# Four of the sixteen chunks of the first two modulation strips multiplied on TensorE with a column of silu(c)

## The reference

```python
c_act = jax.nn.silu(c)                              # (1, 1024)
for l in range(DEPTH):
    mod = c_act @ mod_w[l] + mod_b[l]               # (1, 6 * 1024)
    sh1, sc1, g1, sh2, sc2, g2 = jnp.split(mod, 6, axis=-1)
    h = modulate(x, norm_g[l, 0], sh1, sc1)         # rmsnorm(x) * g * (1 + sc1) + sh1
    y = gla_mixer(h, ...) if l < n_a else swa_sink_attention(h, ...)
    ...
```

## Time and profile before

| | us |
|---|---|
| runs of before (three) | 2585.71, 2585.95, 2589.53 |
| their median | 2585.95 |
| the profiled execution, span from first to last instruction | 2591.7 |
| difference of that span to the median | 5.75 |
| TensorE busy in that span | 2514.7 (97%) |
| VectorE busy | 2119.7 (82%) |
| ACT busy | 1220.0 (47%) |
| mean granted TensorE clock | 0.990 of full |

### The profile page before, as it was taken

One profiled execution on the slowest core, in us unless ns is written; L12 is line 12 of the kernel. 1 busy time (PEld: TensorE's weight loads), 2 busy tenths in 40 slices (PEclk: granted clock), 3 DMA queues, 4 the chain that ended last, 5 costly groups with the idle time before them and its releaser, 6 DMA issues.

```text
span 2591.7 us, 48983 instructions
## 1 busy us (share of the span) xinstructions
PE 2514.7 (97%) x17184; PEld 2192.0 (85%) x17184; DVE 2119.7 (82%) x3783; ACT 1220.0 (47%) x1769; POOL 468.9 (18%) x385
## 2 busy tenths in 40 slices
PE   5999999999999999999999999999999999999998
PEld 4789999888888877899998888887878789777987
DVE  7889997888888778869978888887777788777754
ACT  4544444545444545444444554444545554334543
POOL 2115992000000001018980000000101000110000
PEclk8999999999999999999999999999999999999999
DMA  9775555555456887365555445546887567964554
GB/s 345 259 263 168 179 178 172 166 166 185 169 167 211 284 271 272 130 220 171 183 179 166 162 166 185 170 168 231 282 286 256 189 222 262 318 242 163 171 183 149
DMA packets 147831, 538.38 MB, mean 208 GB/s; under 512 B 16609, under 2 KB 16865, under 8 KB 147442
## 3 DMA queue, kind: packets, MB, share of 16 engines
q1 hardware_dynamic: 114226, 414.78, 46.9%
q0 software_dynamic: 32752, 119.24, 13.2%
q10 hardware_dynamic: 720, 2.62, 0.3%
HBM read 533.42 MB, written 3.15 MB: 207 GB/s over the span
## 4 chain that ended last, share of the span: by engine, by line
PE 83%; DVE 7%; POOL 3%; issue 3%; DMA 2%; ACT 2%; SPq 0%; DVEq 0%; POOLq 0%; ACTq 0%
PE ps L2003 26%; PE ps L1529 9%; PE ps L2748 7%; PE ps L748 6%; PE ps L1505 6%; PE ps L1457 5%; PE ps L1533 5%; PE ps L2730 5%; PE ps L1948 3%; PE ps L1509 3%; POOL split_lo L1575 3%; PE ps L2734 2%; DVE gate L928 1%; DMA gate<-in_mod 1%; PE ps L2142 1%
## 5 line engine op out<-in xcount | busy, mean ns | idle before, releaser
L1562 ACT ACTIVATE split_hi<-ring 128x1024 fp32r<-128x1024 f32 x760 | 801.0, 1056 | 757.8 <-PE ps L1509 199.8
L1587 DVE TENSOR_TENSOR split_lo<-ring,split_hi 128x1024 fp32r<-128x1024 f32 x572 | 698.5, 1222 | 177.0 <-ACT split_hi L1562 172.2
L1575 POOL TENSOR_TENSOR split_lo<-ring,split_hi 128x1024 fp32r<-128x1024 f32 x128 | 339.9, 2672 | 91.2 <-ACT split_hi L1562 90.9
L1559 ACT ACTIVATE gate_hi<-gate 128x256 fp32r (+1 forms) x252 | 105.4, 418 | 405.4 <-PE ps L2003 398.9
L2003 PE MATMUL ps<-split_hi,gate_hi 128*128 128x512 f32 x1024 | 285.1, 398 | 1.5 <-DVE gate_lo L1585 1.5
L2003 PE MATMUL ps<-split_hi,gate_lo 128*128 128x512 f32 x1024 | 278.2, 392 | 5.1 <-DVE gate_lo L1585 5.0
L2003 PE MATMUL ps<-split_lo,gate_hi 128*128 128x512 f32 x1024 | 278.0, 391 | 0.0
L1505 PE MATMUL ps<-h_parts,split_hi 128*128 128x256 f32 x2048 | 266.9, 283 | 0.0
L1529 PE MATMUL ps<-h_parts,split_hi 128*128 128x512 f32 x1024 | 261.6, 397 | 0.0
L1505 PEld LDWEIGHTS ps<-h_parts,split_hi 128*128 128x128 f32 x2048 | 254.9, 192 | 0.0
L2003 PEld LDWEIGHTS ps<-split_hi,gate_lo 128*128 128x128 f32 x1024 | 192.6, 189 | 48.4 <-DVE gate_lo L1585 7.5
(11 more groups left out here) (405 smaller groups left out, 3951.0 us busy)
## 6 DMA issues: line engine op xcount, KB each, us to landing
ring<-in_stream SPq DMA_DIRECT2D x776, 512.0 KB, 4.3
small<-in_mod POOLq DMA_DIRECT2D x104, 512.0 KB, 5.6
mod_w<-in_mod POOLq DMA_DIRECT2D x64, 512.0 KB, 5.2
gate<-in_mod POOLq DMA_DIRECT2D x44, 512.0 KB, 6.9
gate<-in_mod SPq DMA_DIRECT2D x8, 512.0 KB, 16.2
gate<-in_mod ACTq DMA_DIRECT2D x4, 512.0 KB, 8.3
x_kept<-x POOLq DMA_DIRECT2D x8, 256.0 KB, 3.9
gate<-x_kept POOLq DMA_DIRECT2D x4, 512.0 KB, 8.5
```

The source lines that it names most:

```text
L1562: nc.scalar.activation(split_hi[:, e, :], ring[:, slot, e * D:(e + 1) * D], ACT.Copy).then_inc(hi_made, 1)
L1575: nc.gpsimd.tensor_tensor(split_lo[:, e, :], ring[:, slot, e * D:(e + 1) * D], split_hi[:, e, :].bitcast(F32), ALU.subtract).then_inc(lo_m ...
L1587: nc.vector.tensor_tensor(split_lo[:, e, :], ring[:, (START[name] + j) % RING, e * D:(e + 1) * D], split_hi[:, e, :].bitcast(F32), ALU.sub ...
```

## The change

Shift chunks 4 to 7 of the first layer are no longer multiplied by VectorE. The host lays them out transposed, in eight blocks of 128 inputs by 128 outputs. ACT makes a second silu(c), as a column per block (`c_col`, [128, 8]), from eight more columns of the `cols` input; it waits for `cols` between L553 and L554 to do so. TensorE multiplies each block, as stationary weights, with one column of `c_col`, eight products added up in one column of PSUM per chunk. VectorE adds the bias to that column (`shift_bias_vector`) and counts up `first_mod_used`, at the place where the chunk's product stood. On TensorE, chunk 4 stands ahead of the gl products, chunk 5 ahead of gl product 0, chunk 6 ahead of gl product 2, chunk 7 ahead of gl product 4. Chunk 7 shares PSUM bank 7 with chunk 4 and waits until ten chunks are done.

```diff
+SHIFT_ON_VECTOR = 4
...
+        c_col = sb("c_col", [P, 8])
...
+        SHIFT_BANK = {4: 7, 5: 5, 6: 6, 7: 7}
+
+        def shift_chunk_tensor(t, c):
+
+            t.eng.wait_ge(shift_landed[c], 16)
+            t.wait_ge(*when("c_col"))
+            if c == 7:
+                t.eng.wait_ge(first_mod_used, 10)
+            w = shift_mod[:, c, :].rearrange("p (k n) -> p k n", k=DC)
+            for k in range(DC):
+                ins = nc.tensor.matmul(ps[:, SHIFT_BANK[c], c:c + 1], w[:, k, :], c_col[:, k:k + 1],
+                                       start=(k == 0), stop=(k == DC - 1))
+            ins.then_inc(tensor_steps, t.step(f"shift.full{c}"))
+
+        def shift_bias_vector(v, c):
+            v.wait_ge(*when(f"shift.full{c}"))
+            s = PLACE[MOD1[0] + SH1]
+            nc.vector.tensor_tensor(modc[:, s, c:c + 1], ps[:, SHIFT_BANK[c], c:c + 1], mod_b(s, c), ALU.add) \
+                .then_inc(first_mod_used, 1)
...
             nc.scalar.activation(c_row, c_row, ACT.Silu).then_inc(scalar_steps, a.step("c_act"))
+            a.eng.wait_ge(cols_landed, 16)
+            nc.scalar.activation(c_col[:, :], col("cond"), ACT.Silu).then_inc(scalar_steps, a.step("c_col"))
             nc.scalar.activation(c2_row, c2_row, ACT.Silu).then_inc(scalar_steps, a.step("c2_act"))
...
             for c in range(DC):
                 if c >= 4:
                     scale_chunk_vector(v, c)
-                shift_chunk_vector(v, c)
+                if c < SHIFT_ON_VECTOR:
+                    shift_chunk_vector(v, c)
+                else:
+                    shift_bias_vector(v, c)
...
+            shift_chunk_tensor(t, 4)
             for c in range(DC):
+                if c % 2 == 0 and 5 + c // 2 < DC:
+                    shift_chunk_tensor(t, 5 + c // 2)
                 t.wait_ge(*when(f"n1.T{c}"))
                 ins = nc.tensor.matmul(ps[0:16, 4, 0:SEQ], gla_wgl[:, c, :], hT[:, c, :], start=(c == 0), stop=(c == DC - 1))
...
+    for n in range(PLACE[MOD1[0] + SH1] * DC + SHIFT_ON_VECTOR, PLACE[MOD1[0] + SH1] * DC + DC):
+        mod[n] = mod[n].T.reshape(DC, P, P).transpose(1, 0, 2).reshape(P, D)
```

More of the change, by code:

```diff
@@ L109 @@
 for _name, _n in [("mod_b", STRIPS * 8), ("norm1", 32), ("kvn1", 8), ("fin", 8),
-                  ("norm2", 64), ("kvn2", 8), ("b_g2", 4), ("qn", 3), ("kvl", 2), ("pos", 4)]:
+                  ("norm2", 64), ("kvn2", 8), ("b_g2", 4), ("qn", 3), ("kvl", 2), ("cond", 8), ("pos", 4)]:
     COLS[_name] = N_COLS
@@ L3284, in pack @@
         vec(g["norm_g_2"], 8), vec(g["kv_norm_2"], 8), vec(g["gla_b_g2"], 4), vec(g["b_q_norm_2"], 3),
-        vec(g["kv_lora_norm_2"], 2)], axis=1)
+        vec(g["kv_lora_norm_2"], 2), vec(g["c"], 8)], axis=1)
     inv1 = f(500000.0) ** (-np.arange(0, 2 * ROT1, 2, dtype=f) / f(2 * ROT1))
```

## The result

The changed kernel takes 2602.15 us (median of 9; 2595.44 to 2608.56) beside 2586.96 (9; 2584.67 to 2599.78): 1.0045 times the kernel before, interval 1.003 to 1.0061, so 7.8 to 15.8 us. The sign and the mechanism are as forecast; the measured median lies 3.65 us above the range. Measured again beside other kernels it was 2597.96 (12; 2592.89 to 2604.52): 1.004 (1.003 to 1.0051), 7.8 to 13.2 us.

A forecast was written before the change was run, and what follows sets the result against it. Two strands bounded the start: VectorE, ACT, TensorE to 34.96 us, and POOL's inputs to 35.77. TensorE's queue moves the glT copy +8.1 us, less 0.6 for the clock: net +7.5, 2593.5 us, range 2586.5 to 2598.5.

The forecast's parts named there:

- The sign and the mechanism: Whole kernel slower, net +7.5 us, because chunk products on TensorE delay the glT copy from 35.80 to 43.95 us.
- The path: First 45 us: TensorE's queue ends last and releases the glT copy at 43.95 us, no longer the inputs.
- Their price: Chunk products on TensorE: 16 records a chunk, 1.8 us at full clock (0.114 each), 3.4 at half (0.21 each).
- the nearest row: L2472, 128x128 f32 blocks with 8 columns, 0.114 us a record at full clock, taken as the one-column products' price.
- the bounds 1.2 and 5.3: Half-clock chunk price: at least 1.2 us from bf16 records, at most 5.3 us with weights loads that nothing hides.
- chunk 4: 23.98 + 1.8 = 25.8, about all of it at full clock: First step of TensorE's queue: chunk 4 starts at 23.98 us, takes 1.8 us, before the clock falls at about 25.6.
- 4.6 to 4.8 us: Delay from the last close or wide matmuls to the clock's fall, put after transposes ending at 20.93: about 25.6 us.
- Granted is the full 2.4 GHz until about 28.7 us: Clock reading of the kernel before: full until about 28.7 us, then half, 1.2 GHz, until about 45.8.
- the credit of 0.6 us: In `gla_qk`: half clock lasts 4.6 us in place of 5.8, saving 0.6 us.
- rival 2: First 45 us: clock stays full; copy +0.65, z -1.9, `gla_qk` -2.9, together -4.1 us, 2581.8 us; chance 0.12.
- Rivals 1, 3 and 4: Clock falls only at 28.7, +5.7 us (0.10); chunk at bf16 price, +0.9 (0.10); weights load not hidden, +13.2 (0.06).
- the anchor: Median time of the kernel before, 2585.95 us, to which the forecast difference of +7.5 us was added.

The follow-up runs named there:

- e2: Changed kernel with gl products 0 to 3 put ahead of chunks 4 and 5 on TensorE, the rest interleaved; 1.0025 times the kernel before.
- e1: Changed kernel without the TensorE products of shift chunks 4 to 7, which are the bias alone; 1.0001 (0.999 to 1.0012) times the kernel before.
- e11: Changed kernel with each chunk's eight products done twice, 64 in place of 32; 1.0094 (1.008 to 1.0107) times the kernel before.
- e6: Kernel before with unread identity products on TensorE ahead of gl products 4 to 7 and of z; 1.0004 (0.9991 to 1.0017) times the kernel before.
- e5: Changed kernel with unread identity products on TensorE ahead of chunk 4 and between the one-column products; 1.0024 times the kernel before.
- e7: Changed kernel with weights and column of chunks 4 to 7 read as bf16 upper halves; 0.9996 (0.9984 to 1.0008) times the kernel before.
- e9: Changed kernel with only chunks 4 and 5 on TensorE, behind gl product 3, and inputs issued early; 1.0007 (0.9994 to 1.0019) times the kernel before.
- e8: Kernel before with POOL issuing its five small inputs at the eighth product, not the twelfth; 0.9998 (0.9988 to 1.0007) times the kernel before.

## Why the prediction was right, and where it failed

**Right.** The path: the copy released by TensorE, 16 records a chunk. Their price: 3.50 us at half clock against 3.4, 1.95 against 1.8 at full (e2); the nearest row was the right one, the bounds 1.2 and 5.3 were not needed. Gl products 1.81 a pair of c against 1.8. VectorE's idle 13.4 us, over 10. ACT's second silu (0.21 us at 8.84) ends in the shadow of x, awaited to 12.60, and e1 shows that this, the longer `cols` and the new layout together cost nothing that its interval (0.999 to 1.0012) can tell. That a delay before the glT copy reaches the end: e11.

**The step that failed: "chunk 4: 23.98 + 1.8 = 25.8, about all of it at full clock".** The clock did not fall at about 25.6. The stretches of the changed kernel around the start of chunk 4 (24.28), columns as before:

```profile
23.00:24.00 1.00, 0.00 (x0) 0.00 (x0) 0.84 (x2) 0.87 (x2) 0.00 (x0) 0.95 1.02 414
24.00:25.00 1.00, 0.72 (x4) 0.75 (x4) 0.00 (x0) 0.00 (x0) 0.00 (x0) 0.50 1.04 426
...
54.00:55.00 1.00, 1.00 (x8) 1.00 (x7) 0.94 (x3) 0.34 (x2) 0.00 (x0) 0.69 0.92 311
```

A clock of 0.95 over 23 to 24 us and 0.50 behind it is a fall at 23.9, before the first product; in the second profiled execution the same stretch shows

```profile
23.00:24.00 1.00, 0.00 (x0) 0.00 (x0) 0.60 (x2) 0.63 (x2) 0.00 (x0) 0.72 0.98 401
```

so still sooner, about 23.4. Both chunks then ran at half clock, 6.96 us, to 31.2 in place of 29.8. I had carried 4.6 to 4.8 us over from two places where TensorE went on with a few narrow products; here the transposes ended at 20.8 and it did nothing at all until the load landed, 3.48 us by the timeline's bracket. When other products stood in that gap, chunk 4 was at full clock (e2: 1.95 us). That the idle wait is the cause is not shown, though: e11, whose TensorE does the same up to chunk 4, had its fall only at 24.9, inside the chunk,

```profile
24.00:25.00 1.00, 0.68 (x6) 0.71 (x7) 0.00 (x0) 0.00 (x0) 0.00 (x0) 0.96 1.05 430
```

and e0, the kernel before once more, had it 3.7 us after the eight gl records (23.93 to 27.67) where the sum carried over 4.8. With the same work ahead of it the moment moves by more than a microsecond, so it could not be taken from one execution. Behind this lies a reading that failed, "Granted is the full 2.4 GHz until about 28.7 us". The column reads 1.00 from the start on, but the durations do not: the 16 transposes took 3.76 us in before and 3.49 in the second execution of the changed kernel, where the last two records start 0.11 us apart and those ahead of them 0.19 to 0.31. So the clock was at half through most of the transposes and rose only about when they ended, or later; why it fell again so soon stays open.

Of the 1.5 us by which the copy is late (45.49 against 43.95; 45.29 in the second execution) 1.4 stem from here, and chunks 6 and 7 add 0.1 each.

**Twice too large: the credit of 0.6 us** for the clock's return inside `gla_qk`. The half-clock stretch there went from 49.69 to about 54.6 (0.69 over 54 to 55 in the stretches above), 4.9 us in place of 4.6, which by the same working gives 0.4; the chain gives `gla_qk` 24.46 us in place of 24.76, 0.3 less. e6 shows that little more is to be had: with the clock full it waits for gla_lo and for ACT's splits. For the same reason rival 2's -2.9 for `gla_qk` was no gain that e5 or e6 found. Its -1.9 for z came, and most of it was still there at the first `gla_v` product (63.85 us in e6, 65.42 in before, with the copy 0.3 sooner); it went between 113 and 137 us (see Open), and e6's time is 1.0004. The side that rival 2 stood on did not come with a full clock. The Trainium skill, "TensorE: Matmul & The Clock Gate", section "Why this matters for your kernels", advises to leave no idle gaps between bursts of matmuls; e6 filled most of them and had the full clock, without a gain: right behind z TensorE was not what ended last.

**Rivals 1, 3 and 4** fall by the rows: the clock fell sooner, not later; 0.22 us a record is neither the bf16 row's nor that of a weights load that nothing hides. A cheap record came only with bf16 data (e7).

**The range.** With the copy and the credit as measured the working gives 8.1 + 1.5 - 0.3 = 9.3 us (the traces show 9.1 and 9.3 at the PEER query), so 2595.3 on the median given, inside the range. So of the 8.65 us between forecast and measured median, 1.8 are the clock and the credit. The other 6.85, which put it outside the range, lie within the spread of single executions and of the anchor (1.0 of them is the anchor: 2586.96 for nine runs against 2585.95 for three). The second comparison's median, 2597.96, is inside. Medians of the kernel before are 2585.95, 2586.96, 2587.38, 2589.47, 2590.92 and 2591.42, and single executions of it go from 2581 to 2600. Three runs had put the anchor at the low end, and the range had no term for it. What makes single executions differ is settled in part only. The mean granted clock goes with it: in the three groups of 35, 35 and 29 executions of before, the median of those with 0.991 or more lies 4.9 to 6.3 us below that of those with 0.989 or less; in e0's twelve it is 2.3 us. Two profiled spans of the same kernel, 2591.7 and 2585.1, are only 0.5 us apart at the PEER query, so most of it arises later: some 6 us of it between 1780 and 1800 us, where the first of them has TensorE busy for 4.01 of 6 us and then a clock of 0.57 over 8 us, and the second is busy throughout at 1.00.

**Open.** Why the clock fell at 23.4 to 24.9 us, as said. Why e2, e5 and e6 lose some 1.6 us between 113 and 137 us. In e6 the clock falls for a short time there,

```profile
116.00:120.00 4.00, 4.00 (x15) 2.97 (x13) 3.50 (x8) 0.46 (x2) 0.00 (x0) 0.71 0.00 0
```

where the kernel before has 1.00. In e2 and e5 it falls there too (0.65 and 0.61 over 122 to 124 us), and none of the other eleven profiled executions has either the fall or the loss; that the one causes the other was not tried. An exact version that beats the kernel before was not found.

## What to carry to other kernels

Work moved to an engine that looks free in a stretch is priced in that engine's queue: here 32 one-column products stood in front of the products that the path needs, and an f32 product with weights of its own costs about the same for 1 column (0.122 us a record) as for 64 (0.115). Before crediting the relief of the other engine, ask what ends beside it: VectorE's 4.5 us were worth 0.5 at the copy until the inputs moved too. And take neither the clock of a new stretch nor an anchor from few executions: with the same work ahead of it the clock fell at 23.4, 23.9 and 24.9 us, three runs put the median 1.0 to 5.5 us below those of larger groups, and durations are to be read beside the clock column.

## What the runs showed of the hardware that was not expected

- In e2 the clock fell at 27.0 us while TensorE was nearly always busy with one-column f32 products (a single gap of 0.16 us since 24.34). In e5, with pairs of 128-column products between them, it stayed full from 24 to 43 us.
- The granted clock reads 1.00 ahead of its first recorded change whatever the pace. In e9:

```profile
21.50:25.25 3.75, 3.63 (x9) 1.13 (x9) 2.06 (x5) 1.29 (x3) 2.71 (x5) 1.00 1.03 419
```

The eight gl records in it took 3.59 us, 0.45 each, the pace of half clock; the same eight took 1.92 in e2, where everything ahead of them on TensorE is the same, and 3.59 again in e8, also at 1.00. In e7 the column reads 1.00 up to 35 us, over gl products at 1.89 us for four. The Trainium skill, on the page named above, section "What's actually happening", says that the number of slow products at a kernel's start varies from run to run of one kernel; these runs agree with that, and durations tell the pace there, not the clock column.
